# Second pair's values: VectorE evacuates them ahead of a low part of weights, not behind it

## The chip, the cores and the metric

The kernel runs on one core of one Trainium2 chip. The metric is the device time of one execution in microseconds (us), lower is better; it is given as the median of several runs.

## The reference, cut to what matters

Two layers of a decoder. In each layer a mixer (a gated branch A and an attention branch B, merged and projected) is followed by a feed-forward part: dense in the first layer, eight experts in the second. The change lies in branch B's attention over 256 positions, 16 heads of 96 (query and key) and 64 (value) dimensions:

```
q = rms_norm(q, q_norm_g)
k = rms_norm(k, k_norm_g)
...
s = jnp.einsum('bqhd,bkhd->bhqk', q_blk, k, preferred_element_type=jnp.float32) * scale
s = jnp.where(kpos[None, :] <= qpos[:, None], s, jnp.float32(-1e30))
p = jax.nn.softmax(s, axis=-1).astype(v.dtype)
return jnp.einsum('bhqk,bkhd->bqhd', p, v)
```

Everything is float32. Beside the attention stand the projections, `z = h @ w_in`, `A @ P_A`, `B @ P_B` and `merged @ w_out`.

## The kernel before, in words

**Arithmetic.** A float32 product is made of three TensorE passes. Both operands are split into a high part (type fp32r) and a low part (what is left): high by high, high weights by low activations, low weights by high activations. The weights come by DMA in chunks of 128 x 2048 into one of four `raw` buffers (the DMA queue of SyncE waits until the low part of the chunk that used the buffer before is done). For each chunk ScalarE writes `w_hi` (line 507, `Ring.split_hi`), VectorE writes `w_lo` (line 512, `Ring.split_lo`) and TensorE multiplies (line 552). `w_hi` and `w_lo` have three slots.

**The plan.** A list `plan` of steps, written by hand once for both layers, sets the order of work. Each engine walks through the whole list and issues its own part of each step, so its queue has the list's order, and an engine stands at a step until the semaphores of that step have come. A `split` step has a part for ScalarE (`split_hi`) and one for VectorE (`split_lo`); the two names alone issue just one of the parts. A step `split_lo` with chunk n writes the low part of chunk n + 3.

**Attention in slots.** The 16 heads go in eight pairs, and `slot(n)` appends the steps of one slot, each for a different pair: `values` of pair n - 3, `scores` of pair n - 1, `prob_turns` of n - 2, `softmax_max` of n - 1 and, mostly, `softmax` of n - 1. Numbers count from 0: in the fourth slot the values are those of pair 1, the second pair.
- `values`: TensorE multiplies the value rows by the transposed probabilities (lines 936 and 938); ScalarE copies the result out of its PSUM bank as `bt_hi` (line 1252, a helper that copies) and VectorE as `bt_lo` (line 1835), which frees the bank.
- `prob_turns`: TensorE transposes the probabilities into two banks (line 959). Turns use two banks in alternation, and a bank may be written once its last result is read, so the second bank of this step is the one that `bt_lo` frees. ScalarE copies them out as `prob_t`.
- `scores`: lines 950 and 951 on TensorE.
- `softmax_max`: VectorE's row maxima (line 1852, four pieces, then line 1857), which release ScalarE's exponentials (`exps`, `softmax`, line 1377).
- `qk_turns`: TensorE transposes queries and keys (line 972); ScalarE copies them to `qk_t`. The first such step of pairs 4 to 7 waits for `k_scale` of the second half, VectorE's scaling of the keys `kb` (lines 1808 and 1809).

The fourth slot stands behind the second half of the gate projection `gb` 1. Behind the slot come `k_scale` (second half), a low part, `softmax` of pair 3 and the gate's tanh (line 1470); then `pa` 0 (operands `t_hi`, `t_lo`), with the turns of pair 4 after its fourth cell.

Of the kernel before, what the change touches and what calls it, by code (L numbers as in the profile page):

```python
# [58 lines left out]
def decoder_trunk(nc, x, mix_norm_g, w_in, gm_v_norm_g, gm_v_norm_b, gm_w_spatial, gm_b_spatial, gm_w_proj,  # L59
# [31 lines left out]
    chunks = []  # L91
# [16 lines left out]
    def gu_pieces(w_gu, j, k0):  # L108

        v = w_gu.rearrange("(k p) n -> p k n", p=P)  # L110
        return [v[:, k0:k0 + 4, hh * FF + j * HC:hh * FF + (j + 1) * HC] for hh in range(2)]
# [20 lines left out]
    def mul(l, what, j, k0=0, then=(), split=True, inside=()):  # L132

        nonlocal strip_no
        w, c0 = {"cq": (w_in, OFF_CQ), "ckv": (w_in, OFF_CKV), "v": (w_in, OFF_V), "u": (w_in, 0),
                 "ga": (w_in, OFF_GATE), "gb": (w_in, OFF_GATE + D), "uq": (mla_w_uq, 0), "ukv": (mla_w_ukv, 0),
                 "pa": (gm_w_proj, 0), "pb": (mla_w_proj, 0), "wo": (w_out, 0), "gu": (None, 0)}[what]  # L140
        width = KVL + DR if what == "ckv" else STRIP
        if not k0:
            strip_at[l, what, j] = strip_no
            strip_no += 1
        if what == "gu":
            kt, n = KD, 4
            chunks.append((("gu", *gu_pieces(dense_w_gu[l // 2], j, k0)), n, width))
        else:
            v = w[l].rearrange("(k p) n -> p k n", p=P)[:, :, c0 + j * STRIP:c0 + j * STRIP + width]
            kt = v.shape[1]  # L150
            n = min(4, kt - k0)
            h = n // 2
            chunks.append(([(0, h, v[:, k0:k0 + h, :]), (h * width, n - h, v[:, k0 + h:k0 + n, :])], n, width))
        chunk_end[l, what, j] = len(chunks)
        at = 0
        for z, step in inside:
            if z > at:
                plan.append(("mul", l, what, j, k0, n, k0 + n == kt, width, len(chunks) - 1, at, z))
            at = z
            plan.append(step)  # L160
        plan.append(("mul", l, what, j, k0, n, k0 + n == kt, width, len(chunks) - 1, at, TT * n))
        plan.extend(then)
        if split:
            plan.append(("split", l, len(chunks) - 1))

    for l in range(L):
        def evac(what, j=0):
            return "evac", l, what, j

        def slot(n, values=True, exps=True):  # L170
            return ([("values", l, n - 3)] * (n >= 3 and values) + [("scores", l, n - 1)]
                    + [("prob_turns", l, n - 2)] * (n >= 2) + [("softmax_max", l, n - 1)]
                    + [("softmax", l, n - 1)] * exps)

        def split(part="split"):
            return part, l, len(chunks) - 1

        def turn(n):
            return "qk_turns", l, n

        if not l:
# [36 lines left out]
            inside=[(2, ("a_turns", l, 0)), (2, ("softmax", l, 0)), (5, turn(1)), (5, split())])  # L218
        mul(l, "gb", 1, 0, [("values", l, 0), split("split_hi"), *slot(3, values=False, exps=False), ("u_gelu", l, 1),
                            ("branch", l, 1)], split=False, inside=[(4, turn(2)), (4, ("u_tanh", l, 1))])  # L220
        mul(l, "gb", 1, 4, [("split_lo", l, len(chunks) - 2), *slot(4, exps=False), ("k_scale", l, 1), split("split_lo"),
                            ("softmax", l, 3), evac("gb", 1)], split=False,
            inside=[(2, ("exps", l, 2)), (5, ("a_turns", l, 1)), (7, turn(3)), (7, ("norm_probs", l, 2)),
                    (7, split("split_hi"))])
# [14 lines left out]
            split=False)  # L239
# [1911 lines left out]
```

## Time and profile before

| | us |
|---|---|
| median of 3 runs | 1435.34 |
| lowest, highest | 1434.59, 1435.9 |
| the profiled execution | 1435.21 |
| its span, first to last instruction | 1433.4 |
| TensorE busy | 1424.1 |
| VectorE busy | 1143.1 |
| ScalarE busy | 960.6 |

The busy times are sums over the span, and engines work beside each other. The time of an execution is the span and what the launch adds around it. The rows below are of the profiled execution; "PE" is TensorE's matmul, "PEld" its weight load, "DVE" VectorE, "ACT" ScalarE, "SPq" the DMA queue of SyncE. An instruction's time is counted from its start, and the next one on an engine may start a little before it ends.

### The profile page before, as it was taken

What the parts mean: (1) busy time and instruction counts of PE and PEld (TensorE: products, weight loads), DVE (VectorE), ACT (ScalarE), POOL (GpSimd) and SP (SyncE); (2) the same over time, 40 slices, a digit from 0 to 9 for tenths busy, and PEclk for the clock granted to TensorE, in tenths of its full rate; (3) what the DMA queues carried; (4) which work ended last, traced back from release to release, by engine and by line L of the source; (5) the groups of instructions that cost most, each with busy time, mean ns of one, the idle gap of its engine ahead of it and who ended that gap; (6) DMA issues with size and microseconds to landing.
All of it is one profiled execution on the core that took longest, in us unless ns stands there. A gap on an engine that the chain in (4) does not pass through costs nothing.

```text
span 1433.4 us, 19210 instructions
## 1 busy us (share of the span) xinstructions
PE 1424.1 (99%) x6747; PEld 1178.6 (82%) x6747; DVE 1143.1 (80%) x1160; ACT 960.6 (67%) x1003; POOL 45.3 (3%) x54
## 2 busy tenths in 40 slices
PE   9999999999999999999999999999999999999998
PEld 7888778888888888778888888888888888888886
DVE  6987756665547977756989898898898988989986
ACT  6676754544435676754677787777777777777775
POOL 2000003000000000000200000000000000000200
PEclk9999999999999999999999999999999999999999
DMA  9473348955465473447899999999999999999994
GB/s 338 162 236 118 119 157 305 332 177 178 159 214 187 149 234 118 136 159 276 290 352 414 410 359 411 380 386 409 366 402 380 380 412 372 382 386 413 372 397 161
DMA packets 163268, 415.14 MB, mean 290 GB/s; under 512 B 15420, under 2 KB 43960, under 8 KB 163176
## 3 DMA queue, kind: packets, MB, share of 16 engines
q1 hardware_dynamic: 157128, 393.42, 74.7%
q0 software_dynamic: 5008, 16.97, 3.6%
q10 hardware_dynamic: 1040, 3.68, 0.6%
q8 instruction: 39, 0.64, 0.2%
q14 instruction: 53, 0.43, 0.1%
HBM read 398.20 MB, written 15.81 MB: 289 GB/s over the span
## 4 chain that ended last, share of the span: by engine, by line
PE 96%; ACT 2%; DVE 2%; issue 0%; POOL 0%; DVEq 0%; ACTq 0%; POOLq 0%
PE ps L552 88%; PE ps L1109 1%; PE ps L829 1%; PE ps L972 1%; PE ps L951 1%; PE ps L873 1%; PE ps L959 1%; ACT w_hi L507 1%; ACT qk_t L1252 1%; PE ps L938 0%; PE ps L907 0%; PE ps L950 0%; ACT prob L1377 0%; ACT sq L1377 0%; PE ps L846 0%
## 5 line engine op out<-in xcount | busy, mean ns | idle before, releaser
L512 DVE TENSOR_TENSOR w_lo<-raw,w_hi 128x2048 fp32r<-128x2048 f32 (+3 forms) x240 | 500.9, 2105 | 139.2 <-ACT w_hi L507 136.5
L507 ACT ACTIVATE w_hi<-raw 128x2048 fp32r<-128x2048 f32 (+3 forms) x240 | 421.9, 1769 | 187.2 <-PE ps L552 171.5
L552 PE MATMUL ps<-w_hi,act_hi 128*128 128x512 f32 (+1 forms) x1264 | 333.8, 392 | 0.1
L552 PE MATMUL ps<-w_hi,act_lo 128*128 128x512 f32 (+1 forms) x1264 | 331.3, 388 | 0.0
L552 PE MATMUL ps<-w_lo,act_hi 128*128 128x512 f32 (+1 forms) x1264 | 327.4, 387 | 0.0
L552 PEld LDWEIGHTS ps<-w_lo,act_hi 128*128 128x128 f32 x1264 | 235.6, 188 | 48.1
L552 PEld LDWEIGHTS ps<-w_hi,act_lo 128*128 128x128 f32 x1264 | 234.9, 188 | 47.8 <-DVE act_lo L1621 0.2
L552 PEld LDWEIGHTS ps<-w_hi,act_hi 128*128 128x128 f32 x1264 | 232.3, 188 | 46.0 <-ACT act_hi L1252 0.5
L512 DVE TENSOR_TENSOR w_lo<-raw_more,w_hi 128x2048 fp32r<-128x2048 f32 (+1 forms) x96 | 201.9, 2111 | 30.3 <-ACT w_hi L507 30.2
L507 ACT ACTIVATE w_hi<-raw_more 128x2048 fp32r<-128x2048 f32 (+1 forms) x96 | 170.0, 1775 | 55.4 <-PE ps L552 54.4
L512 DVE TENSOR_TENSOR w_lo<-raw_low,w_hi 128x2048 fp32r<-128x2048 f32 (+1 forms) x64 | 137.6, 2156 | 11.2 <-ACT w_hi L507 10.7
L507 ACT ACTIVATE w_hi<-raw_low 128x2048 fp32r<-128x2048 f32 (+1 forms) x64 | 115.9, 1810 | 36.1 <-PE ps L552 35.2
L552 PE MATMUL ps<-w_hi,ehid_hi 128*128 128x512 f32 x352 | 96.6, 392 | 0.0
L552 PE MATMUL ps<-w_hi,ehid_lo 128*128 128x512 f32 x352 | 95.7, 389 | 0.0
L552 PE MATMUL ps<-w_lo,ehid_hi 128*128 128x512 f32 x352 | 95.6, 389 | 0.0
L552 PEld LDWEIGHTS ps<-w_hi,ehid_lo 128*128 128x128 f32 x352 | 66.1, 188 | 13.8
L552 PEld LDWEIGHTS ps<-w_lo,ehid_hi 128*128 128x128 f32 x352 | 66.1, 188 | 13.7
L552 PEld LDWEIGHTS ps<-w_hi,ehid_hi 128*128 128x128 f32 x352 | 65.4, 188 | 13.1
L552 PE MATMUL ps<-w_hi,t_lo 128*128 128x512 f32 x144 | 38.4, 395 | 0.0
L1539 ACT ACTIVATE esig<-ps 128x1024 f32<-128x1024 f32 (+1 forms) x24 | 23.0, 957 | 22.8 <-PE ps L552 22.8
L552 PE MATMUL ps<-w_hi,t_hi 128*128 128x512 f32 x144 | 37.0, 395 | 0.0
L552 PE MATMUL ps<-w_lo,t_hi 128*128 128x512 f32 x144 | 36.3, 390 | 0.0
(285 smaller groups left out, 1232.0 us busy)
## 6 DMA issues: line engine op xcount, KB each, us to landing
raw<-in_moe_w_gu SPq DMA_DIRECT2D x128, 512.0 KB, 9.3
raw_more<-in_moe_w_down SPq DMA_DIRECT2D x80, 512.0 KB, 7.4
raw<-in_w_in SPq DMA_DIRECT2D x72, 512.0 KB, 4.7
raw_low<-in_moe_w_gu SPq DMA_DIRECT2D x64, 512.0 KB, 10.6
raw_more<-in_moe_w_gu SPq DMA_DIRECT2D x64, 512.0 KB, 10.8
raw<-in_moe_w_gu SPq DMA_DIRECT2D x64, 384.0 KB, 7.7
raw<-in_moe_w_down SPq DMA_DIRECT2D x48, 512.0 KB, 7.1
raw<-in_dense_w_gu SPq DMA_DIRECT2D x44, 512.0 KB, 5.0
```

The source lines that it names most:

```text
L507: nc.scalar.activation(w_hi[:, self.split_slot(j), 0:n], self.raw(j)[:, 0:n], ACT.Copy).then_inc(self.hi, 1)
L512: nc.vector.tensor_tensor(w_lo[:, c, 0:n], self.raw(j)[:, 0:n], w_hi[:, c, 0:n].bitcast(F32), ALU.subtract).then_inc(self.lo, 1)
L552: return nc.tensor.matmul(dst, a, b, start=start and n == 0, stop=stop and n == 2)
L829: mm = nc.tensor.transpose(bank[:, i * P:(i + 1) * P], src(i // TT, i % TT), ident)
L873: mm = nc.tensor.transpose(banks[b][:, (k * TT + t) * P:(k * TT + t + 1) * P], xres[:, t, c:c + P], ident)
L951: mm = nc.tensor.matmul(ps[:, 7, hh * S:(hh + 1) * S], q_t[:, P:S], k_t, start=True, stop=True)
L959: mm = nc.tensor.transpose(bank[:, q * P:(q + 1) * P], probs[pair % 2][:, blk * P:(blk + 1) * P], ident)
L972: mm = nc.tensor.transpose(bank[0:DQ, q * P:(q + 1) * P], src[:, q % 2, 2 * pair + hh, :], ident)
L1109: mm = nc.tensor.transpose(turn_banks(j)[:, k * P:(k + 1) * P], ehid[:, k * P:(k + 1) * P], ident)
L1252: return nc.scalar.activation(dst, src, ACT.Copy, scale=scale)
L1539: nc.scalar.activation(esig[:, 0:w], strip_bank(j)[:, 0:w], ACT.Silu).then_inc(z["sig_ready"], 1)
```

## The change

One step changes its place in the list: `values` of pair 1 stood inside the fourth slot, behind a `split_lo`; now it stands ahead of it.

```diff
-        mul(l, "gb", 1, 4, [("split_lo", l, len(chunks) - 2), *slot(4, exps=False), ("k_scale", l, 1), split("split_lo"),
+        mul(l, "gb", 1, 4, [("values", l, 1), ("split_lo", l, len(chunks) - 2), *slot(4, values=False, exps=False), ("k_scale", l, 1), split("split_lo"),
                             ("softmax", l, 3), evac("gb", 1)], split=False,
```

Only VectorE has a part in both steps, so only its queue changes, once in each layer. On VectorE, behind the fourth slot's multiplication, the first layer (the names in brackets are the semaphores that an instruction waits for):

```order
 L1867 TENSOR_TENSOR prob<-prob,soft 128x256 [waits dve_own]
 L1868 TENSOR_TENSOR prob<-prob,soft 128x512
-L512 TENSOR_TENSOR w_lo<-raw,w_hi 128x2048 [waits hi_done]
-L1835 TENSOR_TENSOR bt_lo<-ps,bt_hi 128x256 [waits turn_hi]
+L1835 TENSOR_TENSOR bt_lo<-ps,bt_hi 128x256 [waits turn_hi]
+L512 TENSOR_TENSOR w_lo<-raw,w_hi 128x2048 [waits hi_done]
 L1852 ISA sq,soft<-ps,causal 128x128 [waits scores_done,prob_ready,turn_done]
 L1852 ISA soft 128x1
```

The two neighbours have changed places; `w_lo` is the low part of the first `pa` 0 chunk. Behind the maxima, still on VectorE, the rows are those of before and in the same order:

```order
L1857 SCALAR_TENSOR_TENSOR soft<-soft,q_sum 128x4 [waits dve_own]
L1808 TENSOR_TENSOR kb<-kb,k_sum 128x2x8x64
L1809 TENSOR_TENSOR kb<-kr,k_sum 128x2x8x32
L512 TENSOR_TENSOR w_lo<-raw,w_hi 128x2048 [waits hi_done]
L1866 RECIPROCAL soft<-soft 128x4 [waits exp_done]
```

None of them moved against the others. On TensorE, whose queue is the same in both kernels, the place that waits for `kb` lies inside the first chunk of `pa` 0:

```order
L552 MATMUL ps<-w_hi,t_lo 128x512 [waits turn_free1,turn_free0]
L552 MATMUL ps<-w_hi,t_lo 128x512 x3
L972 MATMUL ps<-consts,qb 96x128 [waits turn_free1,k_ready]
L972 MATMUL ps<-consts,qb 96x128
L972 MATMUL ps<-consts,kb 96x128 x2
L972 MATMUL ps<-consts,qb 96x128 [waits turn_free0]
L972 MATMUL ps<-consts,qb 96x128
L972 MATMUL ps<-consts,kb 96x128 x2
L552 MATMUL ps<-w_hi,t_lo 128x512 x4
L552 MATMUL ps<-w_lo,t_hi 128x512 [waits lo_done]
```

`k_ready` is what line 1809 signals; nothing here moved.

## Rows read from the trace of the kernel before

**Rows 1.** The page, busy time, share of the span and instructions of each engine

```profile
PE 1424.1 (99%) x6747; PEld 1178.6 (82%) x6747; DVE 1143.1 (80%) x1160; ACT 960.6 (67%) x1003; POOL 45.3 (3%) x54
```

**Rows 2.** TensorE's waits: us in total, times, longest; the whole span

```profile
PE ps L846 <- POOL consts L753: 1.8, 1, 1.8
...
PE ps L959 <- DVE bt_lo L1835: 0.3, 2, 0.2
```

**Rows 3.** Timeline, VectorE, first layer: start, duration, instruction, [idle before <-releaser]

```profile
147.66 2.28 DVE L512 TENSOR_TENSOR w_lo<-raw,w_hi 128x2048 fp32r<-128x2048 f32 x1
...
150.49 0.42 DVE L1835 TENSOR_TENSOR bt_lo<-ps,bt_hi 128x256 fp32r<-128x256 f32 x1 [0.54 <-ACT bt_hi L1252]
150.83 0.28 DVE L1852 CUSTOM_DVE_ANT_0 sq<-ps,causal 128x128 f32<-128x128 f32 x1
...
153.27 0.68 DVE L1809 TENSOR_TENSOR kb<-kr,k_sum 128x512 f32<-128x512 f32 x1
153.87 2.28 DVE L512 TENSOR_TENSOR w_lo<-raw,w_hi 128x2048 fp32r<-128x2048 f32 x1
...
156.07 0.17 DVE L1866 RECIPROCAL soft<-soft 128x4 f32<-128x4 f32 x1
```

**Rows 4.** Timeline, ScalarE and the DMA queue of SyncE, first layer

```profile
148.27 1.92 ACT L507 ACTIVATE w_hi<-raw 128x2048 fp32r<-128x2048 f32 x1
...
149.98 7.08 SPq L498 DMA_DIRECT2D raw<-in_gm_w_proj  x4
...
150.07 0.38 ACT L1252 ACTIVATE bt_hi<-ps 128x256 fp32r<-128x256 f32 x1
...
155.53 0.46 ACT L1252 ACTIVATE qk_t<-ps,qk_gain 96x256 f32<-96x256 f32 x1
...
173.20 1.90 ACT L507 ACTIVATE w_hi<-raw 128x2048 fp32r<-128x2048 f32 x1
```

**Rows 5.** Timeline, TensorE and its weight loads, first layer

```profile
148.46 0.39 PE L936 MATMUL ps<-prob_t,vv 128*64 128x128 f32 x4
...
150.97 0.44 PE L959 MATMUL ps<-consts,prob 128*128 128x128 f32 x2 [0.17 <-DVE bt_lo L1835]
...
153.07 1.07 PE L552 MATMUL ps<-w_hi,t_lo 128*128 128x512 f32 x4
...
154.00 0.17 PEld L972 LDWEIGHTS ps<-consts,qb 128*96 128x96 f32 x2 [0.29 <-DVE kb L1809]
154.01 0.42 PE L972 MATMUL ps<-consts,qb 128*96 128x128 f32 x2
...
155.84 1.99 PE L552 MATMUL ps<-w_lo,t_hi 128*128 128x512 f32 x8
```

**Rows 6.** Timeline, the same place in the second layer

```profile
577.82 0.39 ACT L1252 ACTIVATE bt_hi<-ps 128x256 fp32r<-128x256 f32 x1
...
578.24 0.42 DVE L1835 TENSOR_TENSOR bt_lo<-ps,bt_hi 128x256 fp32r<-128x256 f32 x1 [0.53 <-ACT bt_hi L1252]
...
581.02 0.68 DVE L1809 TENSOR_TENSOR kb<-kr,k_sum 128x512 f32<-128x512 f32 x1
...
581.76 0.17 PEld L972 LDWEIGHTS ps<-consts,qb 128*96 128x96 f32 x2 [0.25 <-DVE kb L1809]
```

**Rows 7.** TensorE's last matmuls, then stretches: busy times, PEclk (granted clock), DMA

```profile
1425.81 1.93 PE L1146 MATMUL ps<-y_sb,put 128*128 128x512 f32 x4
...
1429.00:1430.00 1.00, 0.00 (x0) 0.00 (x0) 0.00 (x0) 0.00 (x0) 0.00 (x0) 0.97 1.02 365
1430.00:1431.00 1.00, 0.00 (x0) 0.00 (x0) 0.00 (x0) 0.00 (x0) 0.00 (x0) 0.50 0.24 82
```

**Rows 8.** Transposes of line 846, from 0 to 6, then from 676 to 683 us: ns minimum/median/maximum

```profile
L846 PE MATMUL ps<-consts x12: 421/421/476, 1.8 to 4.2; 128*128 128x128 f32 x12
...
L846 PE MATMUL ps<-consts x22: 272/273/328, 678.7 to 682.6; 128*128 128x128 f32 x22
```

## The prediction

> **What bounds the kernel now.** First the page's busy times: TensorE is busy 1424.1 of 1433.4 us [rows 1], so 9.3 us are idle. 1.80 us of that lie ahead of its first instruction [rows 2] and 5.7 us behind its last matmul, which ends at 1425.81 + 1.93 = 1427.74 [rows 7]. Some 1.8 us are left between, so time anywhere on TensorE's queue is time of the kernel, and a stall put into it has almost nothing later to vanish in. Second, the list of waits: the one that the moved instruction causes, the value transposes' bank (line 959 behind bt_lo), is 0.3 us in 2 places, one in each layer [rows 2]. That is the most an earlier bt_lo could remove by this view. Third, the timeline around the place, engine by engine, since an average says nothing of a swap of two neighbours on VectorE.
>
> There the reader is to see this. VectorE starts the low part w_lo at 147.66, and the next time that it does anything is bt_lo at 150.49, with 0.54 us idle before it, released by ScalarE's bt_hi [rows 3]. ScalarE makes bt_hi late, at 150.07 for 0.38 us, since its own queue has the high part w_hi (148.27, 1.92 us) ahead of it [rows 4]; TensorE had the values ready at 148.46 + 0.39 = 148.85 [rows 5]. So w_lo is done for free: it fills the wait for bt_hi, and VectorE still idles behind it.
>
> **The change, part by part.** On VectorE bt_lo now comes first and w_lo behind it, once in each layer. Nothing is added or removed, and the queues of ScalarE, TensorE, GpSimd and the DMA queue have the same rows as before.
>
> bt_lo: what releases it is bt_hi, whose end (150.07 + 0.38 = 150.45) hangs on ScalarE's order, which is unchanged. It cannot start before 150.49, as before. So the bank comes free at the same time, and line 959 starts its last two transposes at 150.97 as before: gain 0.
>
> w_lo: it now starts at bt_lo's successor place, 150.83, where the first of the row maxima (line 1852) stood [rows 3]. What it costs there is the distance from a w_lo to a waiting successor: 153.87 to 156.07 is 2.20 us [rows 3]. So the maxima start at 153.03, and all that is queued behind them moves by 2.20: the maxima's four pieces and the scale (line 1857), then k_scale (lines 1808 and 1809), whose second part ends at 153.27 + 0.68 = 153.95 before and 156.15 after. VectorE idles from about 147.7 to 150.49 instead.
>
> Who waits for k_scale: TensorE's turns of the fifth pair (line 972). They start at 154.01 before, 0.06 us behind its end, and the weight load ahead of them already waits 0.29 us for kb [rows 5]. The four matmuls ahead of them end at 153.07 + 1.07 = 154.14 [rows 5], so TensorE has nothing in hand and there is no slack: after, the turns start at 156.21. The matmuls behind them (four of w_hi,t_lo, eight of w_lo,t_hi) are in the same queue, so nothing covers it: **2.20 us a layer**.
>
> What is late beside that, and hidden. The maxima's other reader is ScalarE's exponentials, 2.20 later; they and the gate's tanh end at 155.53 before [rows 4], when the first copy of qk_t starts; at 157.73 after, when TensorE too is 2.20 later, so the distance between them stays as it was. The low part itself ends at 153.11 where it ended at 149.94; its reader, the matmuls w_lo,t_hi, stood at 155.84 [rows 5] and will be at 158.0: covered by 4.9 us. The DMA of the slot that it frees is issued at 149.98 [rows 4], now about 153.1; the pair of loads that this row merges lands by 157.06, so at worst 3.2 later, 160.3. ScalarE splits the chunk in question at 173.20 [rows 4]: covered by over 12 us. If that cover were gone, the 3.2 us would be the price. The low part after it (153.87) moves by 2.20 with its reader.
>
> The second layer is the same picture: bt_hi 577.82 + 0.39, bt_lo 578.24 with 0.53 idle before it, k_scale's end at 581.02 + 0.68 = 581.70, weight load at 581.76 with 0.25 us of wait for kb [rows 6]. Another 2.20.
>
> **The sum**: 2 x 2.20 = 4.40 us. The profiled execution took 1435.21 us (span 1433.4) and the median of the three runs is 1435.34, so the profile is 0.13 us from it, and I add to the median: 1435.34 + 4.40 = **1439.7 us**, slower by 0.31%. The bounds: below, the stalls could be given back only out of the 1.8 us that TensorE idles between its ends, which gives 1435.34 + 2.6 = 1437.9; taking all of it is unlikely, for these are waits on engines that run late with it. Above, see the clock.
>
> **The clock.** The granted clock is at its full level (2.4 GHz) through the middle of the kernel. At the end it stands at 0.97 in the stretch 1429 to 1430 and at 0.50 (1.2 GHz) in the next one, and TensorE had been idle since 1427.74 [rows 7]: some 2.2 us. The stall forecast here is also 2.2 us, so that one row says that a fall is possible at each of the two places. The price, from rows at either level: a transpose of line 846 takes 421 ns at the start and 272 ns in the second layer [rows 8], and the slow pace at the start holds at most from 1.80 to some 6.5 us; that long at half the work is 2.4 us. The Trainium skill, TensorE: Matmul & The Clock Gate, Part 1, says that an engine left idle is put back to the lower level and has to earn the higher one by sustained work; the trace's end agrees (0.50 after the idle end). By that rule, if it acts on this stall, the sum is that of the second rival; if not, it is the forecast.
>
> **The rivals.**
> 1. The clock falls in the stall of one layer or both. For: the 2.2 us at the end. Against: there nothing at all followed, and the low level was granted only when the idle time was complete; here work surrounds the stall. Price: 1.2 to 2.4 us for each fall beside the 4.4, so 1441 to 1442.1 for one, up to 1444.5 for two.
> 2. The stall is given back in part, so that under 2.87 us are left. For: 1.8 us of idle time lie between TensorE's ends. Against: TensorE's waits in the list are on VectorE and ScalarE, which are as late as it is. Time: 1437.9.
> 3. It does what its words say: the bank is free earlier and the transposes of line 959 no longer wait. It needs bt_hi ahead of VectorE's free moment. The balance point: VectorE can take bt_lo and then w_lo and still start the maxima at 150.83 only if bt_hi ends by 150.83 - 2.20 - 0.34 - 0.04 = 148.25; it ends at 150.45, and even the values behind it are ready only at 148.85. Were it to hold, TensorE would gain the 0.3 us of line 959 and at most the kb waits of 0.29 and 0.25 [rows 5, 6]: 1434.5. That is not slower.
> 4. The change doesn't reach the chip's order. The order of VectorE's queue shows the swap in both layers, and each instruction there waits in its place; time 1435.3.
>
> **How the numbers follow.** Forecast 0.65; rival 1 0.23 (slower too); rival 2 0.08; rivals 3 and 4 together 0.04. What a measurement of this kernel can tell from no change is about 0.2%, 2.9 us, so 1438.2 divides same from slower. Slower: 0.65 + 0.23 and a little of rival 2, 0.90; same 0.09; faster by over 0.2% 0.01, since not even rival 3 gets there. The range goes from 1437.9, the bound of rival 2, to 1442.8, which takes one fall of the clock in and the double one out.
>
> **What the profile after would show.** TensorE's wait for kb at line 972 at some 2.2 us more, twice, and its busy time unchanged but for modelled ends; bt_lo's wait for bt_hi at 2.7 us in both layers instead of 0.54; w_lo directly behind bt_lo; the first maximum 2.5 us behind bt_lo's start instead of 0.34; the wait of line 959 for bt_lo unchanged. Wrong would be: bt_hi earlier on ScalarE, line 972 at its old time, or a wait on TensorE elsewhere that is shorter than before by some us. A granted clock under 1.00 in the stretches just behind 156 or 584 us would be rival 1.

## The result: 1440.0 us against 1435.6

The changed kernel takes 1440.02 us (median of 9 runs, 1438.79 to 1441.56), the kernel before 1435.59 us (9 runs beside them, 1434.59 to 1435.90). The ratio is 1.0032, 95% interval 1.0024 to 1.0040: slower by 4.4 us. The profiled execution of the changed kernel is its second fastest, 1438.93 us with a span of 1437.2.

TensorE's list of waits (us in total, times, longest) has a new line on top; the line of rows 2 for the bank stands as it was. A second new line, the third here, belongs to the start of the kernel, 7 us in, and has nothing to do with the change (last section):

```profile
PE ps L972 <- DVE kb L1809: 4.1, 2, 2.1
PE ps L846 <- POOL consts L753: 1.8, 1, 1.8
...
PE ps L552 <- DVE w_hi L1708: 0.4, 1, 0.4
PE ps L959 <- DVE bt_lo L1835: 0.3, 2, 0.2
```

The timeline of the first layer, where [rows 3 to 5] were read:

```profile
148.11 1.92 ACT L507 ACTIVATE w_hi<-raw 128x2048 fp32r<-128x2048 f32 x1
...
149.91 0.39 ACT L1252 ACTIVATE bt_hi<-ps 128x256 fp32r<-128x256 f32 x1
...
150.33 0.42 DVE L1835 TENSOR_TENSOR bt_lo<-ps,bt_hi 128x256 fp32r<-128x256 f32 x1 [2.73 <-ACT bt_hi L1252]
...
150.67 2.28 DVE L512 TENSOR_TENSOR w_lo<-raw,w_hi 128x2048 fp32r<-128x2048 f32 x1
...
150.81 0.44 PE L959 MATMUL ps<-consts,prob 128*128 128x128 f32 x2 [0.18 <-DVE bt_lo L1835]
...
152.87 0.28 DVE L1852 CUSTOM_DVE_ANT_0 sq<-ps,causal 128x128 f32<-128x128 f32 x1
...
152.98 6.13 SPq L498 DMA_DIRECT2D raw<-in_gm_w_proj  x4
...
155.31 0.69 DVE L1809 TENSOR_TENSOR kb<-kr,k_sum 128x512 f32<-128x512 f32 x1
...
156.05 0.42 PE L972 MATMUL ps<-consts,qb 128*96 128x128 f32 x2 [2.04 <-DVE kb L1809]
```

All is 0.16 us earlier than before up to bt_lo (it comes from the start of the kernel, last section). With that taken off, bt_lo, the copy ahead of it and line 959 stand where they stood, VectorE's wait for bt_hi has grown from 0.54 to 2.73 us, and the first maximum starts 2.54 us behind bt_lo's start instead of 0.34: 2.20 later. k_scale ends 2.20 later and the turns of line 972 start 2.20 later (156.05 + 0.16 against 154.01). The second layer, to be laid beside [rows 6]:

```profile
580.30 0.43 DVE L1835 TENSOR_TENSOR bt_lo<-ps,bt_hi 128x256 fp32r<-128x256 f32 x1 [2.74 <-ACT bt_hi L1252]
...
586.02 0.42 PE L972 MATMUL ps<-consts,qb 128*96 128x128 f32 x2 [2.07 <-DVE kb L1809]
```

It adds the same again, and the last matmuls show that nothing is given back: they start at 1430.21, where they started at 1425.81 [rows 7], 4.40 us later. (To the hundredth this is chance: the 0.16 us of the start are missing from it, and 0.15 us come in between the second stall and the end, 1430.21 - 586.02 = 844.19 us against 1425.81 - 581.77 = 844.04.)

```profile
1430.21 1.93 PE L1146 MATMUL ps<-y_sb,put 128*128 128x512 f32 x4
```

The two profiled executions differ by only 3.7 us all the same, since the span behind the last matmul was 5.1 us here and 5.7 in the kernel before (1437.2 - 1432.14, 1433.4 - 1427.74). In the other traces below it is 5.0 to 5.5 us, so a difference of two single executions is uncertain by about half a microsecond at that end alone.

### The profile page after: what moved, and what is told of

Its sections match the earlier page's. It is cut to its first block, busy times and chain, and to the rows that moved or that the text cites. A ratio compares the mean times of both kernels' runs of the same rounds, so it can differ in the third digit from the quotient of the medians.

```text
span 1437.2 us, 19210 instructions
## 1 busy us (share of the span) xinstructions
PE 1424.0 (99%) x6747; PEld 1178.1 (82%) x6747; DVE 1143.1 (80%) x1160; ACT 961.2 (67%) x1003; POOL 47.3 (3%) x54
## 4 chain that ended last, share of the span: by engine, by line
PE 95%; DVE 2%; ACT 2%; issue 0%; DMA 0%; SPq 0%; DVEq 0%; ACTq 0%
PE ps L552 88%; PE ps L1109 1%; PE ps L829 1%; PE ps L972 1%; PE ps L951 1%; ACT w_hi L507 1%; ACT qk_t L1252 0%; PE ps L938 0%; DVE w_lo L512 0%; PE ps L907 0%; PE ps L959 0%; PE ps L950 0%; PE ps L873 0%; DMA raw<-in_w_in 0%; DVE sq L1852 0%
```

## The experiments

All edits are against the list of steps behind the second half of `gb` 1, unless something else is said. "Changed" is the kernel after. Each group has its own runs of the kernel before beside it: 1435.30 us (first group: one layer each, low part behind the keys, bt_hi first; one of its 33 executions took 2409.75 us, which doesn't move the median), 1435.41 (second group: bt_hi first with the old order, filled stall, two low parts with and without filling) and 1435.36 (third group: changed again, filled again, keys in the gap). The traces don't start alike: by the second pair's values (line 936, at 148.46 in the kernel before) they are up to 0.32 us earlier or 0.29 later, before anything that was edited. Where a time of one is laid beside another, this is taken off.

**One layer at a time.** The swap in the first layer only (`== 0`), and in the second only (`== 1`).

```diff
-[("values", l, 1), ("split_lo", l, len(chunks) - 2), *slot(4, values=False, exps=False),
+[*([("values", l, 1), ("split_lo", l, len(chunks) - 2)] if l == 0 else
+   [("split_lo", l, len(chunks) - 2), ("values", l, 1)]), *slot(4, values=False, exps=False),
```

> Swap in the first layer only. Theory (VectorE waits 2.7 us for bt_hi at bt_lo, the low part then pushes the maxima, k_scale and so TensorE's turns of line 972 by 2.20 us in each layer, and nothing gives it back): kernel before + 2.2 us = 1437.8. The wait for kb on TensorE is 2.1 us once, near 156 us, and the second layer's place is as before. Rival (only one layer's stall lasts, the other is absorbed): 1435.6 or 1440.0.

> Swap in the second layer only. Theory: kernel before + 2.2 us = 1437.8, the same as with the first layer only; the sum of the two differences is the whole change's 4.4. Rival (a stall in the last layer is absorbed by the router and the experts' loads, or the two stalls interact): under 1 us or over 3.

Measured: first layer 1438.56 us (11 runs, 1437.0 to 1439.71; ratio 1.0021, 1.0012 to 1.0030), second layer 1437.08 (11 runs, 1436.72 to 1439.62; 1.0016, 1.0007 to 1.0025). Each trace has the wait for kb once, 2.1 us. In the traces the distance from line 936 to line 972 grows by 2.20 and 2.18 us in the edited layer and not in the other, and against those values the last matmuls are 2.3 us late in both, so no stall is absorbed. The differences of the medians are 3.3 and 1.8 us, 5.0 together. That they are not 2.2 each has a reason which the next experiments make likely: the executions of the first kernel fall into two groups, 1437.0 to 1437.6 (5 of 11) and 1438.6 to 1439.7 (6 of 11), while the second has 9 of 11 under 1437.9. The lower groups are 1.4 to 2.5 us over the kernel before. No trace was taken of an execution of an upper group; of the eight executions in them (6 and 2) five have a mean granted clock of 0.998 or 0.997, three have the 0.999 that the kernel before has too.

**The low part elsewhere.** The early values stay, the low part goes behind k_scale.

```diff
-[("values", l, 1), ("split_lo", l, len(chunks) - 2), *slot(4, values=False, exps=False), ("k_scale", l, 1), split("split_lo"),
+[*slot(4, exps=False), ("k_scale", l, 1), ("split_lo", l, len(chunks) - 2), split("split_lo"),
```

> The values' evacuation stays ahead, but the low part goes behind the maxima and k_scale instead of directly behind bt_lo. Theory (the price is the low part's place ahead of the maxima, not the early bt_lo): the maxima start 0.34 us behind bt_lo again, k_scale ends as in the kernel before; the low part ends at 156.2 where its matmuls stood at 155.84, so TensorE waits 0.3 to 0.4 us a layer there: 1436.0 to 1436.6. Rival (VectorE waiting for bt_hi at bt_lo is what costs): 1440.

Measured: 1436.03 us (11 runs; ratio 1.0005, 0.9996 to 1.0014). Its trace, first layer:

```profile
150.65 0.42 DVE L1835 TENSOR_TENSOR bt_lo<-ps,bt_hi 128x256 fp32r<-128x256 f32 x1 [2.74 <-ACT bt_hi L1252]
150.99 0.28 DVE L1852 CUSTOM_DVE_ANT_0 sq<-ps,causal 128x128 f32<-128x128 f32 x1
...
156.37 2.09 PE L552 MATMUL ps<-w_lo,t_hi 128*128 128x512 f32 x8 [0.20 <-DVE w_lo L512]
```

VectorE still waits 2.74 us at bt_lo, and that costs nothing; what costs 4 us is the low part between bt_lo and the maxima. Behind the keys it comes late for its own matmuls: the list counts 0.20 us, from the modelled end of the ones ahead, but their start is 0.37 us later (156.37 less the 0.16 by which this trace runs late, against 155.84 [rows 5]), within the 0.3 to 0.4 expected. From the turns of line 972 to the values of the second layer's slot it is 422.67 us instead of 422.20, and the median is 0.7 us up for the two layers.

**Moving what bt_lo waits for.** The changed kernel, with ScalarE's `split_hi` behind the values and not ahead of them.

```diff
-[("values", l, 1), ("split_lo", l, len(chunks) - 2),
+[("values", l, 1), split("split_hi"), ("split_lo", l, len(chunks) - 2),
...
-                    (7, split("split_hi"))])
+                    ])
```

> The changed kernel, with ScalarE's bt_hi ahead of the high part w_hi in its queue. Theory (the balance point: the stall is bt_hi's end + 0.04 + 0.34 + 2.20 less 150.83): bt_hi now ends at 149.25, so the maxima start at 151.83, 1.0 us later than in the kernel before, and TensorE loses 1.0 us a layer: 1437.6; the 0.2 us wait of line 959 for bt_lo is gone but doesn't count, since k_scale comes last. Rival (the cost is the low part beside something else, whatever bt_hi does): 1440.

Measured: 1437.90 us (11 runs, 1436.88 to 1438.19; ratio 1.0015, 1.0006 to 1.0024). In the trace, which runs 0.18 us late by its values, ScalarE now waits for them and bt_hi ends at 149.46:

```profile
149.08 0.38 ACT L1252 ACTIVATE bt_hi<-ps 128x256 fp32r<-128x256 f32 x1 [0.51 <-PE ps L936]
...
149.50 0.42 DVE L1835 TENSOR_TENSOR bt_lo<-ps,bt_hi 128x256 fp32r<-128x256 f32 x1 [1.57 <-ACT bt_hi L1252]
149.84 2.28 DVE L512 TENSOR_TENSOR w_lo<-raw,w_hi 128x2048 fp32r<-128x2048 f32 x1
152.03 0.28 DVE L1852 CUSTOM_DVE_ANT_0 sq<-ps,causal 128x128 f32<-128x128 f32 x1
...
155.22 0.42 PE L972 MATMUL ps<-consts,qb 128*96 128x128 f32 x2 [1.27 <-DVE kb L1809]
```

With the 0.18 us taken off, bt_hi ends at 149.28 and the maxima start at 151.85, where 149.25 and 151.83 were expected: the balance point's sum, with its own terms, is 149.28 + 0.04 + 0.34 + 2.20 = 151.86. The turns start 1.03 us later than in the kernel before (155.22 - 0.18 against 154.01) and not 2.20; in the second layer it is 1.01. (The list says 1.27 us because TensorE, which no longer waits for the bank at line 959, arrives sooner.) So the price of the change is set by the end of bt_hi. The median is 2.6 us up, where 2 x 1.03 would be 2.1; what makes up the rest isn't shown.

**The same with the old order**, low part, then bt_lo:

```diff
-[("split_lo", l, len(chunks) - 2), *slot(4, exps=False),
+[("split_lo", l, len(chunks) - 2), ("values", l, 1), split("split_hi"), *slot(4, values=False, exps=False),
...
-                    (7, split("split_hi"))])
+                    ])
```

> The kernel before, low part ahead of bt_lo, with ScalarE's bt_hi ahead of the high part. Theory: bt_lo starts right behind the low part at 149.9, the maxima at the end of the scores, 150.4, the wait of line 959 for bt_lo (0.17 us) goes, and what is left is 0.2 us a layer: 1435.2, no more than 0.4 us faster than before. Rival (bt_lo's late end is worth more than its wait shows): 1434 or lower.

Measured: 1434.62 us (11 runs, 1433.91 to 1435.63; ratio 0.9996, 0.9987 to 1.0005): 0.8 us under the kernel before, more than the 0.4 expected, but the interval holds no change as well. The bank's wait at line 959 is gone from TensorE's list. In the trace, which runs 0.29 us late by its values, the turns of line 972 stand at 154.01 all the same, and in the second layer the distance is 0.30 us shorter too: 0.6 us in both. More from an earlier bt_lo did not show.

**The stall filled.** The changed kernel, and on TensorE 16 transposes of nothing in front of the wait for the keys.

```diff
+                    if pair == 4: turn_bank(b0), keep_busy(16, 4 + b0 % 2)
                     if pair % 4 == 0:
                         pe.wait_ge(k_ready, 2 * l + pair // 4 + 1)
```

> The changed kernel with 16 transposes of nothing (1.8 us at 0.112 us each) on TensorE in front of its wait for the keys of the fifth pair, into the bank that it writes next. They lie inside the stall, so they cost nothing. If the granted clock falls in some executions behind the stall, the slow end of the changed kernel's times (1441.0 to 1441.6, granted clock 0.998) goes and all executions lie within 1438.8 to 1440.1. Rival (the spread has nothing to do with the stall): the spread is as before, 1438.8 to 1441.6.

> The changed kernel once more, beside its filled version on the same chip. Theory: 1439.4 to 1440.1 median, with some executions over 1440.9 and a granted clock of 0.998 in those (the clock falls in one of the two stalls in some executions), the fastest at 1438.7. Rival (the slow ones were an accident of the first chip): all within 1.3 us, as the kernel before.

> The changed kernel with the 16 transposes in each stall, again. Theory: a spread no wider than the kernel before's, 1438.6 to 1440.2, median 0.3 to 0.9 us under the unfilled one, none with 0.998. Rival: no difference in the median.

Measured: filled 1439.17 us (8 runs, 1438.63 to 1440.42; ratio 1.0027) and again 1439.27 (7 runs, 1438.79 to 1440.13; 1.0028, 1.0016 to 1.0039); changed again, beside the second of them, 1441.71 (5 runs, 1438.88 to 1442.62; 1.0041, 1.0027 to 1.0055). Of the 14 executions of the changed kernel 6 are over 1440.9, and those are the ones with a mean granted clock of 0.998 or 0.997; all others have 0.999. Of the 15 filled ones none is over 1440.5 or under 0.999. The median of the second five was expected at 1439.4 to 1440.1 and missed that, since three of the five have the low mean clock; so the filling is worth 2.4 us in that group and not the 0.3 to 0.9 expected, and 0.8 in the first (1440.0 less 1439.2, two groups that did not run side by side). In the trace (0.32 us early by its values) the filling leaves the turns where the keys put them, at 155.89 + 0.32 = 156.21:

```profile
153.70 1.91 PE L846 MATMUL ps<-consts 128*128 128x128 f32 x16
155.89 0.42 PE L973 MATMUL ps<-consts,qb 128*96 128x128 f32 x2 [0.28 <-DVE kb L1809]
```

So the stall has two prices. The wait alone costs 3.8 and 3.9 us in the medians (1439.17 - 1435.41, 1439.27 - 1435.36); the clock adds nothing in somewhat more than half of the executions, and the others lie 1.9 to 3.4 us over the filled kernel's 1439.2.

**The cause doubled**, both low parts ahead of the maxima, and the same with 35 transposes in each stall.

```diff
-[("values", l, 1), ("split_lo", l, len(chunks) - 2), *slot(4, values=False, exps=False), ("k_scale", l, 1), split("split_lo"),
+[("values", l, 1), ("split_lo", l, len(chunks) - 2), split("split_lo"), *slot(4, values=False, exps=False), ("k_scale", l, 1),
```

> The cause doubled: both low parts stand between bt_lo and the maxima. Theory: the stall is 4.4 us a layer, 8.8 us in both, but the second low part no longer stands ahead of the softmax of pair 3 behind k_scale; 1435.6 + 8.8 = 1444.4 without the clock. Clock theory: TensorE idle for 4.4 us makes the granted clock fall in at least one layer in every execution, with a record of it and 1 to 2.4 us more for each fall: 1445.5 to 1449. Rival (the stall saturates, since TensorE finds other waits): under 1443.

> The doubled cause with 35 transposes of nothing (3.9 us) in each of the two stalls. Clock theory: granted clock full throughout, 1444.4; the difference to the doubled cause without them is the price of the clock. Rival (clock plays no part): the same time as without them.

Measured: 1447.56 us (5 runs, 1446.96 to 1449.15; ratio 1.0087, 1.0073 to 1.0101) and, filled, 1443.62 (5 runs, 1442.94 to 1444.96; 1.0058, 1.0044 to 1.0072). The wait for kb in the trace of the first is 8.5 us in 2 places: twice a low part, twice the stall. Filled, it is 8.2 us over the kernel before against a forecast of 8.8, and in its trace, whose values stand where they stood before, the last matmuls start 8.80 us later (1434.61 against 1425.81). The unfilled one loses 3.9 us more, and its granted clock, in stretches of 2 us (PE, PEld, DVE, ACT and POOL busy, then PEclk), says why:

```profile
156.00:158.00 2.00, 0.00 (x0) 0.00 (x0) 1.97 (x7) 1.16 (x5) 0.00 (x0) 0.66 1.03 387
158.00:160.00 2.00, 1.41 (x7) 1.35 (x8) 1.40 (x4) 2.00 (x6) 0.00 (x0) 0.50 0.81 241
160.00:162.00 2.00, 2.00 (x7) 1.65 (x6) 0.34 (x1) 2.00 (x6) 0.00 (x0) 0.50 0.61 236
162.00:164.00 2.00, 2.00 (x7) 1.58 (x6) 0.00 (x0) 1.26 (x1) 0.00 (x0) 0.63 0.05 20
...
590.00:592.00 2.00, 0.00 (x0) 0.00 (x0) 1.97 (x10) 0.72 (x3) 0.00 (x0) 1.00 0.97 367
592.00:594.00 2.00, 0.96 (x7) 0.95 (x8) 1.40 (x4) 2.00 (x8) 0.00 (x0) 0.89 0.96 262
594.00:596.00 2.00, 2.00 (x7) 1.65 (x6) 0.78 (x2) 2.00 (x7) 0.00 (x0) 0.50 0.78 300
```

In the first layer it falls inside the stall, in the second only behind it: it reads 1.00 while TensorE stands still, and the turns that start at 593.04 begin at full pace. Each time it stays low over the next matmuls. From the turns to the values of the next slot TensorE needs 164.63 - 158.59 = 6.04 us and 598.39 - 593.04 = 5.35, where the changed kernel's first profile has 159.82 - 156.05 = 3.77: 2.3 and 1.6 us for the two falls. Filled, the clock is 1.00 over the same stretches.

**One more execution of the changed kernel**, for its granted clock.

> One more look at the changed kernel, for a record of the granted clock in the stall. If this execution is one of the slow ones (8 of 25 so far were over 1440.9): a stretch at 0.50 behind 155 or 585 us, and its matmuls there at half the pace; the loss is 1.7 to 2.4 us against 1439. If it is a fast one: 1.00 throughout, and the clock's fall in a stall of 2.2 us rests on the mean clock of the executions and on the doubled stall.

(The count in this expectation is wrong; it was 6 of 14.) Measured: one execution, 1440.99 us, mean clock 0.998. The waits for kb are 2.04 us in each layer, as in the first profile of the changed kernel. Stretches of both layers:

```profile
155.00:157.00 2.00, 0.51 (x5) 0.51 (x6) 2.00 (x3) 2.00 (x9) 0.00 (x0) 1.00 0.95 310
157.00:159.00 2.00, 2.00 (x10) 1.65 (x8) 1.97 (x3) 2.00 (x6) 0.00 (x0) 0.63 0.48 187
159.00:161.00 2.00, 2.00 (x6) 1.58 (x5) 0.79 (x2) 2.00 (x3) 0.00 (x0) 0.52 0.44 100
...
587.00:589.00 2.00, 0.94 (x9) 0.94 (x10) 2.00 (x3) 2.00 (x7) 0.00 (x0) 1.00 0.94 352
589.00:591.00 2.00, 2.00 (x11) 1.66 (x10) 1.97 (x4) 2.00 (x7) 0.00 (x0) 1.00 0.23 89
```

and its matmuls behind the first stall, then behind the second:

```profile
156.49 0.42 PE L972 MATMUL ps<-consts,qb 128*96 128x128 f32 x2 [2.04 <-DVE kb L1809]
...
157.33 1.91 PE L552 MATMUL ps<-w_hi,t_lo 128*128 128x512 f32 x4
159.03 2.88 PE L552 MATMUL ps<-w_lo,t_hi 128*128 128x512 f32 x8
161.84 0.65 PE L938 MATMUL ps<-prob_t,vv 128*64 128x256 f32 x4
...
588.07 0.43 PE L972 MATMUL ps<-consts,qb 128*96 128x128 f32 x2 [2.04 <-DVE kb L1809]
...
589.91 1.99 PE L552 MATMUL ps<-w_lo,t_hi 128*128 128x512 f32 x8
```

Behind the first stall the granted clock is at its lower level (1.2 GHz) for a time. It isn't yet at 157.00, half a microsecond after TensorE is at work again; four matmuls of w_hi,t_lo from 157.33 on then take 1.91 us, against 1.17 in the first profile. From the turns to the values of the next slot TensorE needs 161.84 - 156.49 = 5.35 us against the 3.77: a fall costs 1.6 us. Behind the second, an idle time of the same length, it stays at 2.4 GHz. So a stall of 2 us may or may not bring a fall, in one and the same execution.

**Keys in the gap.** What VectorE's wait for bt_hi can hold for free, with bt_hi early, is tried on the kernel before:

```diff
-[("split_lo", l, len(chunks) - 2), *slot(4, exps=False), ("k_scale", l, 1), split("split_lo"),
+[("k_scale", l, 1), ("values", l, 1), split("split_hi"), *slot(4, values=False, exps=False),
+ ("split_lo", l, len(chunks) - 2), split("split_lo"),
...
-                    (7, split("split_hi"))])
+                    ])
```

> VectorE's wait for bt_hi filled with k_scale instead of a low part, bt_hi ahead of the high part on ScalarE, both low parts behind the maxima. Theory: k_scale ends at 149.6, so TensorE's turns of line 972 wait for nothing, nor does line 959; the low part of the first pa chunk ends by 154.3, ahead of its matmuls at 155.7; 0.3 us a layer under the kernel before at most: 1434.3 to 1434.9. Rival (the low part at that place makes TensorE wait, as behind k_scale in the third experiment): 1435.4 or more.

Measured: 1434.45 us (11 runs, 1433.5 to 1435.38; ratio 0.9993, 0.9984 to 1.0002), 0.9 us under the kernel before, as expected, and not clear of no change. In the trace the turns of line 972 come 0.40 us earlier against the values, in each layer. TensorE's list of waits has neither line 972 nor line 959 nor the low part in it.

## Why the prediction was right

**What bounds the kernel.** Right. A stall put into TensorE's queue came out at the last matmul whole: 4.40 us there, and 8.80 for the doubled one with the stall filled.

**bt_lo gains nothing.** Right, and shown twice: line 959 waits for it as before, and when bt_hi was really made early, with the old order, the whole gain was 0.8 us. The bound that rival 3 was given, 1434.5, is about where both kernels with an early bt_hi and no stall came out (1434.62 and 1434.45).

**2.20 us for the low part.** Right in place and size: 2.54 - 0.34 us at the maxima, 2.20 at the turns, in both layers; taken out of that place it left 0.7 us over the kernel before, doubled it gave a wait of 8.5 us. The list of waits says 2.04 and 2.07 for the same stalls, since it counts from the modelled ends of the matmuls ahead. The distance from line 936 to line 972 is 2.19 to 2.21 us longer in both layers of every trace of the changed kernel, filled or not.

**What was said to be hidden.** The low part's end, its DMA (issued at 152.98, the merged loads landed by 159.11) and ScalarE's exponentials cost nothing, as said.

**The sum.** 4.40 was forecast, 4.43 measured. That they agree so closely is in part luck: 4.43 is the median of nine executions of which three have the low mean clock, which the 4.40 doesn't allow for, and the five of the third group, of which three have it too, have a median of 1441.7, 6.35 us over the kernel before. The wait alone, measured with the stall filled, is 3.8 to 3.9 us in the medians. On TensorE's queue it is 2 x 2.20 us in every trace, so the half microsecond that the medians lack isn't in the stalls; the start and the end of the executions vary by as much, and the intervals of the ratios are 0.001 (1.4 us) to either side.

**The clock.** This is where the prediction was off in kind. It took "the clock falls" and "it doesn't" as two cases for the kernel, 0.23 against 0.65. They are two cases for each execution, and both happened: 7 of 15 executions (the single one counted) have the low mean clock, and in one group of runs that made the median 1441.7. The price of 1.2 to 2.4 us a fall was right (1.6 us in one trace, 2.3 and 1.6 in the doubled stall), though not for the reason given: it was worked out from the slow transposes at the start [rows 8], over which the record of the granted clock reads 1.00. The argument against, that work surrounds the stall, was wrong. The row that spoke for it, a fall some 2.2 us behind the last matmul [rows 7], pointed the right way but was one draw: in the first profile of the changed kernel the clock still reads 1.00 in the stretch 1434 to 1435, with TensorE idle since 1432.14, and in that of the swap in the first layer 1.00 in 1433 to 1434, idle since 1429.84. The Trainium skill's rule (TensorE: Matmul & The Clock Gate, Part 1), that an idle engine is put back to the lower level, agrees with the last trace at the first stall, where the fall came behind 2.04 us of idle time; at the second, as long, nothing fell.

**The rivals.** A stall given back in part did not show: the waits before have their old lengths. The bank freed earlier did not show either; its balance point was tested and held. The order on the chip is the changed one, as the timeline shows, which rules out the fourth rival.

## What to carry to other kernels

A low-priority instruction that an in-order engine does while it waits for something else is free only there. Before two neighbours on a queue are swapped, look at what the second of them waits for: if it cannot start earlier, the swap only moves the first one out of its hiding place and in front of all that is queued behind. Where the bounding engine gets an idle time of some 2 us, count the wait and, in part of the executions (7 of 15 here), the slower clock behind it; transposes of nothing in the gap took that second price away here, in all 15 executions with 16 of them.

## What the runs showed of the hardware

The granted clock's answer to an idle time is not the same from one execution to the next, nor between two equal stalls of one execution: 2.04 us of idle time at two places, a fall at one of them. Nor is the moment the same: in the doubled stall (4.27 and 4.24 us idle) it fell inside the first and behind the second, and after the last matmul of a kernel it came 2.2 us behind in one trace and more than 4 in another. At 1.27 us (bt_hi first, 11 runs) no execution had a mean clock under 0.999; that is no proof of no fall, since two of the six long executions of the swap in the first layer have 0.999 as well.

The start varies too, and it set the 0.16 us by which everything stood earlier in the first profile of the changed kernel. There the eight transposes of the input take 1.24 us, with the same start as before, and line 552 then waits for w_hi (start, duration):

```profile
4.77 1.24 PE L873 MATMUL ps<-consts,xres 128*128 128x128 f32 x8
5.84 1.04 PE L846 MATMUL ps<-consts 128*128 128x128 f32 x8
7.25 0.93 PE L552 MATMUL ps<-w_hi,act_hi 128*128 128x512 f32 x3 [0.37 <-DVE w_hi L1708]
```

In the kernel before:

```profile
4.77 1.96 PE L873 MATMUL ps<-consts,xres 128*128 128x128 f32 x8
6.53 1.07 PE L846 MATMUL ps<-consts 128*128 128x128 f32 x8
7.35 0.95 PE L552 MATMUL ps<-w_hi,act_hi 128*128 128x512 f32 x3
```

Of the 0.69 us that the transposes gain, TensorE gives back most while it waits for w_hi: the projection starts 0.10 us earlier, and by the next transposes (9.39 against 9.56) it is 0.17. Over all traces the eight transposes take from 1.10 to 1.97 us. What makes them faster in some isn't shown; the granted clock reads 1.00 from 4 to 6 us in both of these.
